# Two transformer blocks in one kernel: the second block's output projection as three rounded passes on split operands

## The reference, cut to what matters

```python
def second_block(x, ...):
    for l in range(DEPTH):                       # DEPTH = 2
        h = rms_norm(x, attn_pre_norm[l])
        mix = hybrid_mixer(h, ..., w_out[l])     # ends in: mix @ w_out
        x = x + rms_norm(mix, attn_post_norm[l])
        h = rms_norm(x, ffn_pre_norm[l])
        x = x + rms_norm(conv_ffn(h, w_up[l], conv_w[l], conv_b[l], w_down[l]), ffn_post_norm[l])

mix = jnp.concatenate([o_fox.reshape(B, S, -1), o_nsa.reshape(B, S, -1), o_dil.reshape(B, S, -1)], axis=-1)
return mix @ w_out
```

## Time and profile before

| | |
|---|---|
| median of 3 runs | 1774.92 us (1773.42 to 1779.65) |
| the profiled execution: its own time | 1778.55 us |
| its span, first to last instruction | 1776.8 us |
| PE busy | 1701.8 us, 96% |
| DVE busy | 1182.2 us, 67% |
| ACT busy | 836.8 us, 47% |
| POOL busy | 125.4 us, 7% |
| mean granted clock of PE | 0.984 of full |
| HBM read | 321.02 MB, 181 GB/s over the span |

### The profile page before, as it was taken

One profiled execution on the slowest core, in us unless ns is written; L12 is line 12 of the kernel. 1 busy time (PEld: TensorE's weight loads), 2 busy tenths in 40 slices (PEclk: granted clock), 3 DMA queues, 4 the chain that ended last, 5 costly groups with the idle time before them and its releaser, 6 DMA issues. The chain is left out here.

```text
span 1776.8 us, 24717 instructions
## 1 busy us (share of the span) xinstructions
PE 1701.8 (96%) x9275; PEld 1382.9 (78%) x9275; DVE 1182.2 (67%) x2156; ACT 836.8 (47%) x1473; POOL 125.4 (7%) x271
## 2 busy tenths in 40 slices
PE   6899999999999999999999999999999999999998
PEld 3787676689878786774899878657998787569986
DVE  6787555865866975558735676656778757557785
ACT  3335364355443442652455444555554534645553
POOL 1000011000000000210000010130000101310000
PEclk8999999999999999999999999899999998999999
DMA  9787424557855984327556637406555476055652
GB/s 338 271 291 237 143 88 146 184 188 260 296 164 183 345 269 138 119 96 237 175 178 203 191 121 240 140 1 204 153 186 184 142 228 163 1 164 168 182 187 83
DMA packets 185911, 323.70 MB, mean 182 GB/s; under 512 B 13540, under 2 KB 101184, under 8 KB 185792
## 3 DMA queue, kind: packets, MB, share of 16 engines
q1 hardware_dynamic: 183200, 320.54, 55.5%
q10 hardware_dynamic: 2592, 1.57, 0.3%
HBM read 321.02 MB, written 1.05 MB: 181 GB/s over the span
## 5 line engine op out<-in xcount | busy, mean ns | idle before, releaser
L1733 DVE TENSOR_TENSOR ring_r<-ring,high 128x1024 fp32r<-128x1024 f32 (+3 forms) x382 | 451.6, 1196 | 283.8 <-ACT high L1313 275.8
L1313 ACT ACTIVATE high<-ring 128x1024 fp32r<-128x1024 f32 (+3 forms) x382 | 392.8, 1037 | 486.6 <-PE bank L691 354.9
L691 PE MATMUL bank<-ring_r,featT_r 128*128 128x512 f32 (+3 forms) x864 | 330.5, 383 | 0.0
L691 PE MATMUL bank<-featT_r,high 128*128 128x256 f32 x960 | 275.4, 287 | 7.9 <-DVE ring_r L1733 7.9
L691 PE MATMUL bank<-oT_r,high 128*128 128x256 f32 x960 | 274.0, 285 | 0.0
L691 PE MATMUL bank<-featT_r,ring_r 128*128 128x256 f32 x960 | 274.0, 285 | 0.0
L691 PE MATMUL bank<-high,featT_r 128*128 128x512 f32 (+3 forms) x680 | 265.7, 391 | 5.8 <-DVE ring_r L1733 4.1
L691 PE MATMUL bank<-high,oT_r 128*128 128x512 f32 (+3 forms) x680 | 258.0, 379 | 0.0
L691 PE MATMUL bank<-high,gates_r 128*128 128x512 f32 x736 | 229.9, 390 | 3.4 <-DVE ring_r L1733 2.6
L691 PEld LDWEIGHTS bank<-featT_r,high 128*128 128x128 f32 x960 | 186.9, 195 | 9.3 <-issue 8.2
L691 PEld LDWEIGHTS bank<-oT_r,high 128*128 128x128 f32 x960 | 186.8, 195 | 0.3 <-issue 0.2
(11 more groups left out here) (259 smaller groups left out, 2227.2 us busy)
## 6 DMA issues: line engine op xcount, KB each, us to landing
ring<-in_w_ff SPq DMA_DIRECT2D x128, 512.0 KB, 4.6
ring<-in_w_ada SPq DMA_DIRECT2D x96, 512.0 KB, 5.8
ring<-in_w_up SPq DMA_DIRECT2D x176, 256.0 KB, 3.3
ring<-in_w_in SPq DMA_DIRECT2D x64, 464.0 KB, 5.4
ring<-in_w_in SPq DMA_DIRECT2D x48, 512.0 KB, 5.3
ring<-in_w_in SPq DMA_DIRECT2D x48, 474.0 KB, 4.5
ring<-in_w_down SPq DMA_DIRECT2D x44, 512.0 KB, 3.4
ring<-in_w_out SPq DMA_DIRECT2D x24, 512.0 KB, 4.8
```

The source lines that it names most:

```text
L691: ins = pe.matmul(o, a, b, start=start, stop=stop, skip_group_check=True)
L1313: act.activation(it["high"], it["raw"], ACT.Copy).then_inc(high_ready, 1)
L1733: dve.tensor_tensor(it["low"], it["raw"], it["high"].bitcast(F32), ALU.subtract).then_inc(low_ready, 1)
```

## The change

The two units of `w_out_2` are listed by `split_given` instead of `plain`: they are split on ACT and DVE as other weights are. Unit 0's rounded copies go to the four slots of `high`, unit 1's to spare places in `gates` and `big`. The head outputs are written by DVE as a rounded copy (in `featT_r`) and a remainder (`featL`) instead of one float32 copy. On PE `two_as_ready` takes the place of `linear_pair`; it gives 96 rounded matmuls for 32 plain ones, and the transposes of tile 0 stand behind the first piece of the last part instead of behind the second. Transfers and their order are the same.

```diff
+        spare_out_2 = slots(gates_r, 0, PIECE) + slots(big_r, 6 * PIECE, 7 * PIECE)
...
+        def split_given(*pieces, spare=None):
+
+            split_units.append(pieces)
+            low_units.append(pieces)
+            for j, it in enumerate(pieces):
+                put(it, spare[j] if spare else None, False, 12)
+
...
-                plain(cols_piece(w, 0, 2, (cols.start, cols.stop)),
-                      *[piece(2, 512, [(slice(0, HD), all_k, all_n, lower[:, j:j + 2, :]),
-                                       (slice(HD, P), all_k, all_n, upper[:, j:j + 2, :])]) for j in (0, 2)],
-                      cols_piece(w, 6, 8, (cols.start, cols.stop)))
+                split_given(cols_piece(w, 0, 2, (cols.start, cols.stop), split=True),
+                            *[piece(2, 512, [(slice(0, HD), all_k, all_n, lower[:, j:j + 2, :]),
+                                             (slice(HD, P), all_k, all_n, upper[:, j:j + 2, :])], split=True) for j in (0, 2)],
+                            cols_piece(w, 6, 8, (cols.start, cols.stop), split=True), spare=spare_out_2 if u else None)
...
@@ PE @@
-                linear_pair(lambda c, t: oT[:, c, t * P:(t + 1) * P], scaled, (1, 1))
+                two_as_ready({(1, 1, 1): (scaled, 0)}, (for_dve, for_dve, outputs, outputs))
...
@@ ACT @@
                 read(ins)
+                highs(2)
                 turns_out(key_turns + dil_turns)
                 act.preload_act_table_set("natural_log_exp_and_others")
...
                     elif i == 3:
                         seen.more(pc_in)
                         act.activation(pc2[:, :, :, :], pc[:, :, :, :], ACT.Exp).then_inc(pc_exp, 1)
+                        highs(1)
+                    elif i == 4:
+                        highs(1)
...
                 softmax_heads(second_jobs, compressed)
+                highs(4)
+                square_banks(deep_tile0[LAYERS1 + 2 * l], (0, 0), (0, 1))
                 highs(2)
-                square_banks(deep_tile0[LAYERS1 + 2 * l], (0, 0), (0, 1))
                 square_parts((0, 0), (0, 1))
                 highs(2)
...
@@ DVE @@
-                        b = tile(outputs)
-                        read(outputs, dve.tensor_copy(out_view(jobs[i - 4]["chunk"], fill is not None),
-                                                      b[:, 0:S].rearrange("p (t s) -> p t s", t=T)))
+                        b, c = tile(outputs), jobs[i - 4]["chunk"]
+                        if fill is not None:
+                            read(outputs, dve.tensor_copy(out_of(c), b[:, 0:S].rearrange("p (t s) -> p t s", t=T)))
+                        else:
+                            link(dve.tensor_copy(featT_r[:, c, :], b[:, 0:S]))
+                            read(outputs, dve.tensor_tensor(featL[:, c, :], b[:, 0:S], featT_r[:, c, :].bitcast(F32), ALU.subtract))
...
                 link(dve.reciprocal(gn[:, 1, :], gn[:, 1, :]))
+                first_quarters(2)
                 turns_out(key_turns + dil_turns)
...
+                    elif i == 6:
+                        first_quarters(2)
 
                 softmax_heads(second_jobs, compressed)
 
-                first_quarters(2)
+                split_unit()
                 seen.more(bc_loaded, 32)
                 products(0, 0)
                 normed(0)
                 scale_tokens([0])
-                first_quarters(2)
+                first_quarters(3)
                 features_out(pcol[:, 2 + l, 96:104], None, True, [0])
+                first_quarters(1)
                 products(0, 1)
```

More of the change, by code:

```diff
@@ L199, in two_blocks @@
         spare_2 = slots(gates_r, 0, PIECE) + slots(sm_r, PIECE) + slots(pT_r, 0)
+        spare_out_2 = slots(gates_r, 0, PIECE) + slots(big_r, 6 * PIECE, 7 * PIECE)
+        assert T * N_IN <= 6 * PIECE
         spare_gates = slots(oT_r, 8 * S) + slots(kvm_r, PIECE) + slots(gates_r, 5 * PIECE) + [None]
@@ L1905, in gates_out @@
                 read(outputs, dve.tensor_copy(n, b[:, :]))
-            def out_view(c, l1):
-                return out_of(c) if l1 else oT[:, c, :].rearrange("p (t s) -> p t s", t=T)
             def softmax_heads(jobs, beside=None, fill=None):
```

## The result

The changed kernel takes 1790.53 us (median of 4 runs, 1789.56 to 1791.88), the kernel before 1776.43 in the runs beside it. The ratio is 1.0076, with a 95% interval of 1.0063 to 1.0090: slower by 14.1 us. The forecast was 1784.0, slower, with a range up to 1792. The direction and the range held; the sum, +9, was too small by a third of what came, and 1790.53 lies outside the 1780 to 1789 that the forecast gave to its likeliest case.

What follows compares the result with a forecast made beforehand. PE, busy for 96% of the span, was taken to bound the kernel. Per layer -5.45 + 3.1 + 3.5 + 0.45 + 2.9 = +4.5 us, +9 in all, against 1774.92 gives 1784 us, range 1775 to 1792.

Steps and rivals of the forecast that it cites:

- likeliest case: Whole kernel: added waits outweigh the projection's gain, +9 us in all, 1784 us (1780 to 1789); chance 0.60.
- passes of the projection: Projection on PE: 96 rounded matmuls and eight transposes take 22.6 us for 28.05, a gain of 5.45 us a layer.
- wait behind the gelu: Behind the gelu, PE waits for ACT's copies and DVE's subtractions: loss 3.1 us a layer (1.5 to 3.3).
- heads and last cast: Second block's heads: DVE's added subtractions and casts cost PE 3.5 us (1.0 to 4.5), the last one 0.45, a layer.
- tile 0's two waits: Beside the projection: PE waits 0.6 us for tile 0's scaling and 1.0 us for its features, a layer.
- tile 1's features: Behind the projection: one more DVE subtraction ahead of tile 1's chain makes PE wait 1.3 us a layer.
- The casts with the last copy: Heads: 0.45 us more per output bank on DVE, 1.8 less 1.0 of idle time, and 0.45 for the last.
- The pair at step 6: Heads: two DVE subtractions of 2.4 us, with a 0.45 us cast, start DVE's step 6 some 2.85 us late.
- PE stands for 2.9 us: Step 7 of the heads: PE waits 2.9 us for POOL's scaling, held up by DVE's late reciprocals.
- The clock: Rival, heads: longer waits on PE bring further half clock, some 4 us a layer, +17 in all, 1792 us; chance 0.14.
- Covered heads: Rival: step 6's subtractions and the casts are swallowed, heads cost 1.0, +0.3 us a layer, 1775.5 us, no change; chance 0.18.
- All splits covered, faster: Rival: DVE's idle time takes up all subtractions but the last 0.45 us, -5.0 us a layer, 1765 us; chance 0.08.

Runs made afterwards that it cites:

- e2_early: The changed kernel with ACT's first two rounded copies made ahead of the gelu instead of behind it: 1780.19 us, ratio 1.0021.
- e3_both: The changed kernel with ACT's first two copies ahead of the gelu and DVE's pair of subtractions at step 5 instead of 6: 1772.40 us, ratio 0.9976.
- e8_casts: The kernel before, with a linked DVE subtraction into unused space behind each of the eight copies of an output bank: 1778.30 us, ratio 1.0016.
- e1_step5: The changed kernel with DVE's pair of subtractions at the head of step 5 of the heads instead of step 6: 1785.18 us, ratio 1.0047.
- e4_filled: The changed kernel with four unused plain float32 matmuls of 512 columns in PE's wait behind the gelu: 1785.09 us, ratio 1.0050.
- e7_padded: e3_both with one unused 512-column float32 matmul ahead of each of two groups of 15-column matmuls in step 2 of the heads: 1777.31 us, ratio 1.0008.
- e5_order: e3_both with ACT's squares ahead of its copies and one of DVE's three subtractions moved behind tile 0's features: 1772.96 us, ratio 0.9988.
- e6_wait: The kernel before, with three linked unused DVE subtractions ahead of its share of the transposes behind the gelu: 1788.34 us, ratio 1.0077.

## Why the prediction was right, and where its sum fell short

Its terms beside what layer 1 showed:

```
                               forecast   measured
passes of the projection        -5.45      -4.85 (23.93 less the waits of 0.23 and 0.50, from 28.05)
wait behind the gelu            +3.1       +3.0
heads and last cast             +3.95      +5.33 late heads
early heads, clock               0         +3.2
tile 0's two waits              +1.6       +0.73
tile 1's features               +1.3       +0.71
sum of a layer                  +4.5       +8.1
```

**The passes.** Right in kind, 0.6 a layer too favourable. With full clock the 96 passes and the transposes took 23.2 us, not 22.6; the pace read from 23 starts leaves out the joints: by the starts in the trace, 0.34 us behind the first matmul and 0.89 behind the last, of which 0.50 are the wait. Some 0.2 more are lost about the transposes.

**The wait behind the gelu.** Right, with its mechanism: 3.0 for 3.1, ended by DVE's `qz`, nothing covered by DVE's idle time. e2_early shows that the place of two copies on ACT is the whole of it.

**The heads.** The two pieces of the term are confirmed apart. The casts with the last copy cost 1.3 (e3_both) to 1.6 us (e8_casts), forecast 1.7. The pair at step 6 costs 4.0 (e1_step5), forecast 2.4. Its wait was 2.59, the subtractions taking 2.75 (the first, begun while POOL was still scaling, 1.62, the second 1.21) and not 2.4; the other 1.4 came with the half-clock stretch behind it. Without that stretch the late heads are at 3.9, the forecast's 3.95. "PE stands for 2.9 us" was nearly right, the name of the engine that ends the wait was not.

**Beside the projection.** All three waits came at their places and behind the instructions named. They are smaller: 0.23 for 0.6, 0.50 for 1.0, and for tile 1 a wait of 0.40 and 0.7 us in all for 1.3. PE came later than forecast, at 18.0 and 23.4 us of the projection instead of 17.7 and 23.2, and DVE was there at 18.2 and 23.9, the latter 0.3 earlier than worked out. Without the clock the terms come to some +3.5 measured for +4.5 forecast, and even that owes something to luck: the passes were 0.6 too favourable, these three waits 1.5 too dear.

**The clock.** This is the step that failed. For the early heads the forecast took nothing into its sum; that the clock would add some 4 us a layer on top of its terms it held to be a rival, with a chance of 0.14. The rival is what came, not the case that had 0.60: 1790.5 lies beyond the likeliest case's own range (1780 to 1789) and beside the rival's 1792. By the prediction's own signs, too, it is the rival that holds: the clock is 0.65 in the early heads, where well under 0.80 was named, and 0.95 in the late ones, where under 1.00 was. The stated range held because it had been drawn up to the rival's figure. The rival's two causes, the long wait behind the gelu and the new one in step 7, are what was found: +3.2 in the early heads (shown by e4_filled, which leaves the wait and takes away the idleness) and up to 1.4 in the late ones (which go with the wait in e1_step5). By the Trainium skill, page TensorE: Matmul & The Clock Gate, part 1, the half clock is the state to which an idle PE falls back. The traces agree with it for the stretch that begins in the wait behind the gelu, and that is gone when the wait is filled; the one in step 7 begins 1.2 us after its wait has ended. The rule had been cited beside the rival. Since the sum itself made the waits, the clock belonged into the likeliest case.

**The other rivals.** "Covered heads" falls for this kernel, by the gap of 2.59 us. "All splits covered, faster" named the right condition, added waits below 2.8 us a layer: e3_both fulfils it by moving the two pairs to where the idle time is, with 1.3 in the heads and 1.4 behind them, and is faster by 0.24% (0.15% to 0.34%), clear of noise but less than the 0.3% that the prediction called faster, since the passes gave 0.6 less. So the rounded projection is worth a little, and this change's loss is that of two placements.

**Still open.** Why the clock falls to half for some 10 us in the early heads of every kernel here, that of before included, where PE had been busy for 9.12 of the 9.23 us ahead of it. e7_padded only shows that two more dense matmuls don't prevent it. With it goes a scatter: the same instructions gave early heads of 24.66 us at a clock of 0.79 in e3_both and 25.97 at 0.74 in the trace of e5_order, and e8_casts has 25.96 where the kernel before has 25.05. In layer 1 of e5_order and of e8_casts this stretch is 13.6 us long instead of 10.2; in layer 2 of the same two traces it is 10.2, and the early heads take 25.04 and 25.05. So the scatter is one of this stretch's length, and nothing here says what sets it. It is smaller than the 3.2 us of the change, which both layers show.

## What to carry to other kernels

If a split feeds the bounding engine, look for idle time for both of its halves, each in its own engine's in-order list: here the same instructions, moved by one step on DVE and by one call on ACT, turned 0.8% slower into 0.24% faster. Price a new wait on TensorE at its length and again at what the granted clock takes in the next stage: here the added 3.2 us of wait alone cost over 6 a layer (12.7 us in e6_wait). And compare a kernel's stages by busy time and clock together: a bounding engine whose busy time doesn't fall when its work does is one sign of a lower clock, and more idle time behind the half-clock stretch, as in e6_wait, can be another.

## What the runs showed of the hardware

- A wait on PE of 4.4 to 4.7 us (with 8.6 us of busy time ahead of it) was followed by two half-clock stretches, in both layers of the changed kernel, e1_step5 and e6_wait: one that began in the wait or as it ended, 6.8 us long, and another after 3 to 10 us at full clock, of 7 to 14 us. With waits of 1.37 and 1.45 us, and with the wait filled by matmuls, only the second came in the early heads, mostly 10 us long (13.6 in layer 1 of e5_order and e8_casts, 6.8 in layer 2 of e7_padded).
- The half clock's price needn't show as busy time: it was 4.4 us of busy time in the change's early heads, partly given back in smaller waits (idle 1.4 instead of 2.5), but only waits in e6_wait.
- Two subtractions of 128x1024 took 2.36 us behind the gelu, where POOL did nothing, and 2.75 in step 6, begun while POOL was scaling. The other engine can lose more: in e1_step5 and e3_both, where the pair stands beside POOL's four scalings, these took 2.88 us instead of 1.90. The casts of 128x256 from a bank and the subtractions behind them took 0.42 each, as the copy had.
